# Modulation chunks of the Hyena stage: the contraction over four 32-column groups of TensorE, summed by a selection matmul

## The chip, the cores and the metric

One core of one Trainium2 chip. The metric is the device time of one execution in microseconds; a lower number is better. Three runs of the kernel before are given, and one more execution was recorded by the hardware profiler.

## What is computed

One layer of a hybrid diffusion trunk over 1,024 latent and 128 context tokens of width 1,024. The part that matters here is the modulation, a linear map of two conditioning vectors (latent and context) to six rows of width 1,024 each:

```python
def adaln(cond, w_mod, b_mod):
    return jnp.split(jax.nn.silu(cond) @ w_mod + b_mod, 6, axis=-1)
...
proj = h @ p['w_in'][l]     # its last 3 x 512 columns feed the Hyena mixer
uc = up[:, :-2] * short_w[0] + up[:, 1:-1] * short_w[1] + up[:, 2:] * short_w[2] + short_b
```

`silu(cond) @ w_mod` is a product of a 2 x 1024 matrix with a 1024 x 6144 one. All data are float32.

## The kernel before, in words

The program of each engine is written out by hand and ordered by semaphores. SP's queue issues nearly all loads; waits on it hold back what is behind them.

`w_mod` is taken in 24 chunks of 256 columns (`CHUNK`, `MOD_CHUNKS`). The first eight (`COND_CHUNKS`) are done at the start. The other 16, chunks 8 to 23, are done in the second stage, which also projects the 12 Hyena features of 128 channels (`FEATS`) from six chunks of `w_in` of 256 columns. After each pair of features a group of modulation chunks follows: `MODS_AFTER = (3, 3, 3, 3, 2, 2)`.

Every chunk of either matrix is 1 MB and goes through a ring of two places, `wring` (line 222): the place of a chunk comes free when the product two chunks before it is done. `HY_AT` and `MOD_AT` (lines 380, 381) number the ring's chunks in order: one of `w_in`, then the group's chunks of `w_mod`, then the next of `w_in`. In a group of three, here called m0, m1 and m2, SP (lines 457 to 471) loads m0 during the features; m1 once the second feature's product is there, since it takes the `w_in` chunk's place; m2 after m0's product; the next `w_in` chunk after m1's product; the next group's m0 after m2's product. In a group of two the next `w_in` chunk is loaded after m0's product.

On TensorE (lines 1049 to 1067) a feature is 24 calls of `mm` (8 steps of contraction by 512, 512 and 128 tokens). Then the feature before it is transposed to tokens (`to_tokens`), and after an odd feature follow the products of the group. `modulation` (line 934) multiplies eight 128-row slices of `w_mod` by the two-column `cond_silu` into two rows of a PSUM bank (`mod_bank`, line 368), accumulating over the slices. A float32 call appears in the trace as two weight loads and two matmuls, so a chunk is 16 matmuls and a feature is 48.

ScalarE copies the two rows to one of two places of `mod_ring` (`copy_mod`, line 656). Before it takes a place again it waits until the store of the chunk two before it has landed (`mod_stored`, line 659). GpSimd (lines 569 to 581) loads the piece of the bias, adds it, for chunks 16 to 19 adds 1.0 as well (line 579), and issues the store of the row to DRAM. The next feature, which is the first to write banks 0 to 2 again, waits on TensorE for `mod_copied` of the whole group, so for the copy of its last chunk (line 1055). VectorE convolves each feature over the tokens (lines 1532 to 1538), normalises and rotates one tile of queries and keys, and after the last feature goes on to the Fourier transforms of the Hyena mixer.

Of the kernel before, what the change touches and what calls it, by code (L numbers as in the profile page):

```python
# [19 lines left out]
ALU = mybir.AluOpType  # L20
ACT = mybir.ActivationFunctionType
AX = mybir.AxisListType
# [6 lines left out]
KT = D // P  # L29
# [10 lines left out]
CHUNK = 256  # L40
MOD_CHUNKS = 6 * D // CHUNK
COND_CHUNKS = 2 * D // CHUNK
# [4 lines left out]
MODS_AFTER = (3, 3, 3, 3, 2, 2)  # L47
# [100 lines left out]
def build(nc, I, O):  # L148
    ctx = ExitStack()
    with ctx:  # L150
        SB_COLS = 53000
        PS = ctx.enter_context(nc.psum_tensor("PS", [P, 8 * 512], F32))

        def bank(b, width=512, rows=P, at=0):
            return PS[0:rows, 512 * b + at:512 * b + at + width]
# [11 lines left out]
        def sem(name):  # L167
            if name not in sems:
                sems[name] = ctx.enter_context(nc.semaphore(name))
            return sems[name]  # L170


        keep = Columns(nc, 0, 4096)
        tables = keep.take(4 * P + 32)
        ident, ones, upper, row128 = (tables[:, P * i:P * (i + 1)] for i in range(4))
# [10 lines left out]
        cond_silu = keep.take(16, "p (k c) -> p k c", c=2)  # L186
# [3 lines left out]
        hid_cols = keep.take(P)  # L190
        w1_sb = keep.take(HID)
        col_v = keep.take(8)
        col_q = keep.take(8)
        col_t = keep.take(8)
        col_r = keep.take(16, "p (o i) -> p o i", o=2)
# [28 lines left out]
        w3 = low.take(4 * HW)  # L224
# [13 lines left out]
        U = [top.take(NTILE * HW, "p (t n) -> p t n", t=NTILE) for _ in range(3)]  # L238
        TAIL0 = top.at
        uc = top.take(2 * T, "p (r t) -> p r t", r=2)  # L240
        rope = Columns(nc, 50560, SB_COLS)
        rot = rope.take(NLAT * 2 * HD, "p (t s d) -> p t s d", t=NLAT, s=2)
        qk_work = rope.take(640)
        swap = rope.take(640)
# [122 lines left out]

        def mod_bank(c):

            return bank(6 + c % 2, CHUNK, rows=2) if c < COND_CHUNKS else bank(MOD_PLACE[c], CHUNK, rows=2)  # L370

        def mat(cls, kind):

# [7 lines left out]
        MOD_AT = [*range(COND_CHUNKS), *(HY_AT[c] + 1 + i for c in range(HY_CHUNKS) for i in range(MODS_AFTER[c]))]  # L381

        MOD_PLACE = {COND_CHUNKS + sum(MODS_AFTER[:c]) + i: i for c in range(HY_CHUNKS) for i in range(MODS_AFTER[c])}

        def ring(at):
            return wring[:, at % 2, :, :]

        def ring_count(at):
            return 16 * (at // 2 + 1)
# [8 lines left out]
        def _(sp):  # L398
# [51 lines left out]
            def mods_before(c):  # L450
                return COND_CHUNKS + sum(MODS_AFTER[:c])
# [5 lines left out]
            for c in range(HY_CHUNKS):  # L457
                for i in range(MODS_AFTER[c]):
                    m = mods_before(c) + i
                    if i >= 2:  # L460
                        sp.wait_ge(sem("mod_product"), m - 1)
                    elif i == 1:
                        sp.wait_ge(sem("feature_product"), 2 * (c + 1))
                    elif c:
                        sp.wait_ge(sem("mod_product"), m)
                    else:
                        sp.wait_ge(sem("qkv_product"), QKV_CHUNKS * NTILE)
                    load_w_mod(m)
                if c + 1 < HY_CHUNKS:
                    sp.wait_ge(sem("mod_product"), mods_before(c + 1) - 1)  # L470
                    load_w_in(QKV_CHUNKS + c + 1, HY_AT[c + 1])

            for r in range(3):
# [173 lines left out]
        def _(act):  # L647
# [8 lines left out]
            def copy_mod(c):  # L656
                act.wait_ge(sem("mod_product"), c + 1)
                if c >= COND_CHUNKS + 2:
                    act.wait_ge(sem(f"mod_stored{c % 2}"), 16 * ((c - COND_CHUNKS) // 2))
                elif c >= 2:  # L660
                    act.wait_ge(sem(f"cond_stored{c % 2}"), 16 * (c // 2))
                act.copy(mod_ring[0:2, c % 2, :], mod_bank(c)).then_inc(sem("mod_copied"), 1)  # L662
                if c < COND_CHUNKS:
                    act.wait_ge(sem("mod_copied"), c + 1)
                    act.dma_start(mod_d[:, CHUNK * c:CHUNK * (c + 1)], mod_ring[0:2, c % 2, :]).then_inc(
                        sem(f"cond_stored{c % 2}"), 16)

            def hidden(layer):
                act.wait_ge(sem("arg_ready"), layer + 1)
                dst = h1T if layer == 0 else h2T[0:HID, :]  # L670
                act.activation(dst, arg, ACT.Sin).then_inc(sem("sine_ready"), 1)
# [68 lines left out]
            for p in range(PASSES):  # L740
                m = 7 * p
# [23 lines left out]
                        copy_spectrum(p, SPEC_MID + i // 2)  # L765

            def copy_mods(c):
                for i in range(MODS_AFTER[c]):
                    copy_mod(COND_CHUNKS + sum(MODS_AFTER[:c]) + i)

            def square_qk(t):

# [143 lines left out]
        def _(pe):  # L916
# [17 lines left out]
            def modulation(c):  # L934
                at = MOD_AT[c]
                pe.wait_ge(sem(f"w_loaded{at % 2}"), ring_count(at))
                if c >= 2:
                    pe.wait_ge(sem("mod_copied"), c - 1)
                for k in range(KT):
                    last = mm(mod_bank(c), cond_silu[:, k, :], ring(at)[:, k, :], k == 0, k == KT - 1)  # L940
                last.then_inc(sem("mod_product"), 1)

            def taps(p, i):
                n, (j, d), (o, half) = N_ITEMS * p + i, divmod(i, 2), divmod(p, 2)
                if n >= 2:
                    pe.wait_ge(sem("taps_ready"), n - 1)
                mm(taps_bank(n), h2T[:, P * j:P * (j + 1)], w3_taps(o, half, d)).then_inc(sem("taps_product"), 1)
# [63 lines left out]
            for p in range(PASSES):  # L1011
                m = 7 * p
# [22 lines left out]

            pe.wait_ge(sem("spectrum_copied"), PASSES * N_SPEC)
            pe.wait_ge(sem("qkv_copied"), QKV_CHUNKS * NTILE)

            def to_tokens(f):
                pe.wait_ge(sem("conv_ready"), f + 1)  # L1040
# [8 lines left out]
            for f in range(FEATS):  # L1049
                at = HY_AT[f // 2]  # L1050
                b = 3 * (f % 2)
                pe.wait_ge(sem(f"w_loaded{at % 2}"), ring_count(at))
                if f >= 2:
                    pe.wait_ge(sem("conv_ready"), f - 1)
                    pe.wait_ge(sem("mod_copied"), COND_CHUNKS + sum(MODS_AFTER[:f // 2]))
                for part, (t0, t1) in enumerate(((0, 512), (512, 1024), (1024, T))):
                    for k in range(KT):
                        last = mm(bank(b + part, t1 - t0), ring(at)[:, k, P * (f % 2):P * (f % 2 + 1)], xT[:, k, t0:t1],
                                  k == 0, k == KT - 1)
                last.then_inc(sem("feature_product"), 1)  # L1060
                if f:
                    to_tokens(f - 1)
                if f % 2 == 1:
                    pe.wait_ge(sem("conv_ready"), f)
                    first = COND_CHUNKS + sum(MODS_AFTER[:f // 2])
                    for c in range(first, first + MODS_AFTER[f // 2]):
                        modulation(c)
            to_tokens(FEATS - 1)
            pe.wait_ge(sem("mod_copied"), MOD_CHUNKS)
            pe.wait_ge(sem("mats_loaded"), 32)  # L1070
# [52 lines left out]
            for s in range(10):  # L1123
# [8 lines left out]
                for a in range(4):  # L1132
                    last = turn(bank(b + 2, P, at=P * a),
                                k_split[:, s % 2, a // 2, a % 2, :, :].rearrange("p c d -> p (c d)").bitcast(F32))
# [103 lines left out]
            for i in range(2 * NTILE):  # L1238
                last = mm(bank(4, MAX_BLOCKS), r_hot[:, i, :], r_tok[:, i, :], i == 0, i == 2 * NTILE - 1)
# [5 lines left out]
            with pe.Fori(0, pairs) as i:  # L1245
                for u in range(2):
# [4 lines left out]
                    for k in range(KT):  # L1251
                        last = turn(bank(2 * u + k // 4, P, at=P * (k % 4)), xg[:, u, k:D:KT])
                    last.then_inc(sem("x_transposed"), 1)
                for u in range(2):
                    pe.wait_ge(sem("xT_ready"), 2 * i + u + 1)
                    pe.wait_ge(sem(f"we_loaded{u}"), 32 * i + 32)
                    for g in range(2):
                        for s in range(2):
                            for k in range(KT):
                                last = mm(bank(4 + u, P, at=256 * g + P * s), w_gu[:, u, g, k, s:FF:2], xgT[:, u, k, :],  # L1260
                                          k == 0, k == KT - 1)
                    last.then_inc(sem("gate_up_product"), 1)
                for u in range(2):
                    pe.wait_ge(sem(f"wd_loaded{u}"), 16 * i + 16)
                    pe.wait_ge(sem("hidden_ready"), 2 * i + u + 1)
                    for c in range(2):
                        for s in range(2):
                            last = mm(bank((6, 2)[u] + c), hT[:, u, s, :], w_dn[:, u, s, 512 * c:512 * (c + 1)], s == 0, s == 1)
# [3 lines left out]
        def _(dve):  # L1272
            steps = [0]

            def own(ins):

                steps[0] += 1
                ins.then_inc(sem("dve_step"), 1)
                dve.wait_ge(sem("dve_step"), steps[0])
# [3 lines left out]
            def give(ins, name):  # L1283

                counts[name] = counts.get(name, 0) + 1
                ins.then_inc(sem(name), 1)
                dve.wait_ge(sem(name), counts[name])
# [199 lines left out]
                transform_taps(p)  # L1487


            for lc in range(2):  # L1490
                own(dve.tensor_copy(tap_s[:, 0:4, lc, 0:3], taps[:, 0:4, :]))
                own(dve.tensor_copy(tap_s[:, 0:4, lc, 3], tap_bias[:, 0:4]))
                for o in range(2):
                    f = slice(4 * o + 4, 4 * o + 8)
                    r = col_r[:, o, 4 * lc:4 * lc + 4]
                    own(tt(tap_s[:, f, lc, 0:3], taps[:, f, :], r.unsqueeze(2).broadcast_to([P, 4, 3]), ALU.mult))
                    own(tt(tap_s[:, f, lc, 3], tap_bias[:, f], r, ALU.mult))
# [68 lines left out]
            for s in range(10):  # L1566
# [3 lines left out]
                r = s % 2  # L1570
# [200 lines left out]
            for t in range(NTILE):  # L1771
                a, at = acc[:, t % YN, :], 16 * (t % YN)
# [59 lines left out]
```

## Time and profile before

| | us |
|---|---|
| three runs | 2078.23, 2080.09, 2081.88 (median 2080.09) |
| the profiled execution, its own time | 2078.15 |
| span of that execution in the profile | 2076.3 |
| TensorE matmuls busy in the span | 1581.8 (76%) |
| VectorE busy | 1041.8 (50%) |
| ScalarE busy | 399.2 (19%) |
| GpSimd busy | 281.4 (14%) |
| second stage, first feature to last transposition | about 354 to 634 |

The page counts matmuls as PE and weight loads as PEld. PEclk is the clock that TensorE was granted, as a share of 2.4 GHz: 1.00 is that level, 0.50 is 1.2 GHz. In the chain of waits a DMA counts from its issue to its landing. Times of positions are microseconds from the span's start. A time given for a group of modulation chunks below counts from the issue of m1's load, which is when the second feature's product is done.

### The profile page before, as it was taken

Reading aid. Unit: us, or ns where it says so; the run is one execution under the profiler, and the core shown is the slowest. Engines: PE = TensorE matmul, PEld = TensorE weight load, DVE = VectorE, ACT = ScalarE, POOL = GpSimd, SP = SyncE. Lnnn points to the kernel's source line nnn. Section 1 sums busy time; section 2 is a strip of 40 time slices with the busy share of each in tenths; the row PEclk is TensorE's granted clock in tenths of the full one; section 3 lists DMA queues with packets and bytes.
Section 4 is the critical chain, followed back from the end, with each engine's and each line's share of the span. In section 5 each row is a group of like instructions: output and inputs, shape, how many; then the busy total and the mean of one; then the engine's idle time right before and its main releaser. Section 6 shows DMA issues by size and latency. Waiting matters only on the chain.

```text
span 2076.3 us, 21496 instructions
## 1 busy us (share of the span) xinstructions
PE 1581.8 (76%) x7898; PEld 1121.6 (54%) x7898; DVE 1041.8 (50%) x1823; ACT 399.2 (19%) x774; POOL 281.4 (14%) x263
## 2 busy tenths in 40 slices
PE   4798787999993904818988997999539999999800
PEld 1376575444441401317888886455338888788700
DVE  2457655455527598685665666443341111112187
ACT  1542331010000100104333333011001111111021
POOL 0220220111100000000000000245300000001076
PEclk8798898999996956959998997999659999999955
DMA  7311112222222201129300001111148898888542
GB/s 242 128 56 66 46 52 86 82 82 82 81 73 81 78 20 31 61 81 407 139 1 1 1 1 34 68 61 41 51 181 325 338 348 327 346 344 342 219 176 94
DMA packets 98624, 273.79 MB, mean 132 GB/s; under 512 B 9415, under 2 KB 55063, under 8 KB 85048
## 3 DMA queue, kind: packets, MB, share of 16 engines
q1 hardware_dynamic: 72152, 215.07, 28.4%
q10 hardware_dynamic: 17888, 30.43, 3.9%
q0 software_dynamic: 8512, 27.34, 3.5%
q8 instruction: 43, 0.70, 0.1%
q14 instruction: 29, 0.24, 0.0%
HBM read 207.62 MB, written 65.19 MB: 131 GB/s over the span
## 4 chain that ended last, share of the span: by engine, by line
PE 60%; DVE 23%; DMA 6%; POOL 5%; issue 3%; ACT 2%; SPq 0%; ACTq 0%; POOLq 0%; DVEq 0%
PE PS L918 55%; DVE buffer L1290 11%; PE PS L921 5%; DVE buffer L1303 3%; DMA buffer<-in_w_mod 3%; POOL buffer L566 1%; DMA buffer<-in_x_tok 1%; DVE buffer L1636 1%; DVE buffer L1758 1%; POOL buffer L599 1%; POOL buffer L601 1%; POOL buffer L593 1%; POOL buffer L591 1%; DMA buffer<-in_w_in 1%; DVE buffer L1315 1%
## 5 line engine op out<-in xcount | busy, mean ns | idle before, releaser
L918 PE MATMUL PS<-buffer 128*128 128x128 f32 (+6 forms) x6678 | 1435.4, 375 | 295.0 <-DVE buffer L1290 167.3
L918 PEld LDWEIGHTS PS<-buffer 128*128 128x128 f32 (+2 forms) x6678 | 973.3, 194 | 729.4 <-issue 358.3
L1290 DVE TENSOR_TENSOR buffer<-buffer 128x512 f32<-128x512 f32 (+15 forms) x534 | 323.7, 606 | 36.6 <-ACT buffer L787 9.7
L921 PE MATMUL PS<-buffer 128*128 128x128 f32 x1220 | 180.0, 296 | 88.8 <-DVE buffer L1290 67.1
L921 PEld LDWEIGHTS PS<-buffer 128*128 128x128 f32 x1220 | 153.6, 163 | 113.9 <-issue 92.3
L1290 DVE TENSOR_TENSOR buffer<-PS,buffer 128x256 f32<-128x256 f32 (+2 forms) x135 | 97.7, 724 | 139.6 <-PE PS L918 97.3
L1290 DVE TENSOR_TENSOR buffer<-buffer,PS 128x256 f32<-128x256 f32 (+2 forms) x44 | 19.0, 431 | 260.1 <-ACT buffer L885 244.0
L820 ACT ACTIVATE buffer<-PS,buffer 128x1152 f32<-128x1152 f32 (+1 forms) x72 | 81.1, 1127 | 215.9 <-DVE buffer L1584 215.9
L1584 DVE TENSOR_REDUCE buffer<-PS 128x1 f32<-128x1152 f32 (+1 forms) x72 | 89.2, 1240 | 65.0 <-PE PS L918 64.6
L1303 DVE SCALAR_TENSOR_TENSOR buffer<-buffer 128x512 f32<-128x512 f32 (+5 forms) x119 | 111.6, 938 | 4.1
L591 POOL TENSOR_TENSOR buffer<-buffer 128x1024 f32<-128x1024 f32 x9 | 21.1, 2344 | 483.5 <-DVE buffer L1650 483.5
L566 POOL TENSOR_TENSOR buffer<-buffer 128x256 f32<-128x256 f32 x64 | 46.4, 726 | 245.3 <-ACT buffer L697 240.9
L1534 DVE TENSOR_SCALAR buffer<-PS,buffer 128x1024 f32<-128x1024 f32 (+1 forms) x24 | 21.0, 877 | 99.6 <-PE PS L918 99.2
L1767 DVE COPY buffer<-PS 128x512 f32<-128x512 f32 x34 | 23.5, 692 | 90.8 <-PE PS L918 90.8
L885 ACT ACTIVATE buffer<-PS 128x256 f32<-128x256 f32 x34 | 13.1, 384 | 253.2 <-PE PS L918 253.2
L1614 DVE COPY buffer<-PS 128x640 f32<-128x640 f32 x64 | 52.8, 825 | 7.6 <-PE PS L921 5.7
L611 POOL COPY buffer<-buffer 128x1 int32 x34 | 6.3, 186 | 363.0 <-PE PS L921 314.3
L575 POOL TENSOR_TENSOR buffer<-buffer 2x256 f32<-2x256 f32 x16 | 11.4, 714 | 302.3 <-ACT buffer L662 278.8
L787 ACT COPY buffer<-PS 128x512 f32<-128x512 f32 (+1 forms) x36 | 15.2, 481 | 186.8 <-PE PS L921 186.8
L1758 DVE COPY buffer<-PS 128x1024 f32<-128x1024 f32 x34 | 40.1, 1220 | 14.0 <-PE PS L921 14.0
L1630 DVE TENSOR_SCALAR buffer<-PS,buffer 128x128 f32<-128x128 f32 x36 | 12.6, 351 | 65.7 <-PE PS L921 64.7
L705 ACT COPY buffer<-PS 128x256 f32<-128x256 f32 x88 | 32.2, 366 | 65.2 <-PE PS L918 53.1
(104 smaller groups left out, 735.0 us busy)
## 6 DMA issues: line engine op xcount, KB each, us to landing
buffer<-in_exp_w_gate SPq DMA_DIRECT2D x34, 1024.0 KB, 4.8
buffer<-in_exp_w_up SPq DMA_DIRECT2D x34, 1024.0 KB, 6.9
buffer<-in_exp_w_down SPq DMA_DIRECT2D x34, 1024.0 KB, 8.5
slot_outputs<-buffer SPq DMA_DIRECT2D x5, 5120.0 KB, 39.1
buffer<-in_w_mod SPq DMA_DIRECT2D x24, 1024.0 KB, 5.4
slot_outputs<-buffer ACTq DMA_DIRECT2D x34, 512.0 KB, 8.7
filter_spectra<-buffer ACTq DMA_DIRECT2D x88, 128.0 KB, 1.7
buffer<-filter_spectra SPq DMA_DIRECT2D x22, 512.0 KB, 3.6
```

The source lines that it names most:

```text
L566: pool.tensor_tensor(total, total, sq[:, added % 2, :], ALU.add).then_inc(sem("sq_added"), 1)
L591: pool.tensor_tensor(x1[:, t, :], xnorm, ln1_g, ALU.mult).then_inc(sem("pool_step"), 1)
L705: act.copy(spec_out[:, m % 3, :], spec_bank(m)).then_inc(sem("spectrum_copied"), 1)
L820: act.activation(probs[:, i % 2, 0:n], PS[:, 0:n], ACT.Exp, bias=nmax[:, i:i + 1], scale=1.0, accum_out=psums[:, i:i + 1]).then_inc(sem("e ...
L918: return nc.tensor.matmul(out, lhsT, rhs, start=start, stop=stop)
L921: return nc.tensor.transpose(out, in_, ident)
L1290: return dve.tensor_tensor(out, a, b, op)
L1303: own(dve.scalar_tensor_tensor(out, a, s, b, ALU.mult, op))
L1584: give(dve.tensor_reduce(nmax[:, i:i + 1], PS[:, 0:n], AX.X, ALU.max, negate=True), "max_ready")
L1614: give(dve.tensor_copy(probsT[:, i % 2, 4:9, :], PS[:, 2048:2688].rearrange("p (t n) -> p t n", t=5)), "probsT_d")
L1758: dve.tensor_copy(xgT[:, u, :, :], PS[:, 1024 * u:1024 * (u + 1)].rearrange("p (k n) -> p k n", k=KT)).then_inc(sem("xT_ready"), 1)
L1767: dve.tensor_copy(ybuf[:, u, 512:1024], bank((7, 3)[u])).then_inc(sem("y_d"), 1)
```

## The change

Three things are made once on VectorE, ahead of the short-tap scales: `cond_wide`, the conditioning vectors in 8 slices of 32 columns, of which two hold data and 30 are zero; the zeroing itself; and `part_sum`, a 128 x 2 selection matrix that has a one where a partition is 0 or 1 modulo 32. In `modulation_parts` the eight slices of a chunk go to four column groups of the array, two slices to each, so that four partial sums land on partitions 0, 32, 64 and 96 of a bank. ScalarE copies the whole 128 x 256 of partial sums to SBUF (`copy_parts`, into `w3`, which is no longer needed and has room for four chunks in use), and `sum_parts` multiplies them by `part_sum`, which gives the two rows in the second half of the same bank. All partial products of a group come first on TensorE, then all sums; on ScalarE all copies of parts, then all copies of rows. The waits of SP's loads go by the partial products. GpSimd's program stays as it is. `SB_COLS` grows by 200 columns.

```diff
+        part_sum = keep.take(2)
...
-        rope = Columns(nc, 50560, SB_COLS)
+        cond_wide = Columns(nc, 52928, SB_COLS).take(KT * 32, "p (k m) -> p k m", k=KT)
+        rope = Columns(nc, 50560, 52928)
...
-            return bank(6 + c % 2, CHUNK, rows=2) if c < COND_CHUNKS else bank(MOD_PLACE[c], CHUNK, rows=2)
+            return bank(6 + c % 2, CHUNK, rows=2) if c < COND_CHUNKS else bank(MOD_PLACE[c], CHUNK, rows=2, at=CHUNK)
+
+        mod_parts = w3.rearrange("p (r c) -> p r c", r=8)
...
                     if i >= 2:
-                        sp.wait_ge(sem("mod_product"), m - 1)
+                        sp.wait_ge(sem("parts_product"), m - 1 - COND_CHUNKS)
                     elif i == 1:
                         sp.wait_ge(sem("feature_product"), 2 * (c + 1))
                     elif c:
-                        sp.wait_ge(sem("mod_product"), m)
+                        sp.wait_ge(sem("parts_product"), m - COND_CHUNKS)
...
-                    sp.wait_ge(sem("mod_product"), mods_before(c + 1) - 1)
+                    sp.wait_ge(sem("parts_product"), mods_before(c + 1) - 1 - COND_CHUNKS)
...
+            def copy_parts(c):
+                act.wait_ge(sem("parts_product"), c - COND_CHUNKS + 1)
+                if c >= COND_CHUNKS + 4:
+                    act.wait_ge(sem("mod_product"), c - 3)
+                act.copy(mod_parts[:, c % 4, :], bank(MOD_PLACE[c], CHUNK)).then_inc(sem("parts_copied"), 1)
...
             def copy_mods(c):
-                for i in range(MODS_AFTER[c]):
-                    copy_mod(COND_CHUNKS + sum(MODS_AFTER[:c]) + i)
+                first = COND_CHUNKS + sum(MODS_AFTER[:c])
+                for m in range(first, first + MODS_AFTER[c]):
+                    copy_parts(m)
+                for m in range(first, first + MODS_AFTER[c]):
+                    copy_mod(m)
...
+            def modulation_parts(c):
+                at = MOD_AT[c]
+                pe.wait_ge(sem(f"w_loaded{at % 2}"), ring_count(at))
+                for half in range(2):
+                    for j in range(4):
+                        k = 2 * j + half
+                        last = nc.tensor.matmul(PS[32 * j:32 * j + 32, 512 * MOD_PLACE[c]:512 * MOD_PLACE[c] + CHUNK],
+                                                cond_wide[:, k, :], ring(at)[:, k, :], start=half == 0, stop=half == 1,
+                                                tile_position=(0, 32 * j))
+                last.then_inc(sem("parts_product"), 1)
+
+            def sum_parts(c):
+                pe.wait_ge(sem("parts_copied"), c - COND_CHUNKS + 1)
+                mm(mod_bank(c), part_sum, mod_parts[:, c % 4, :]).then_inc(sem("mod_product"), 1)
...
+            pe.wait_ge(sem("cond_wide_ready"), 1)
...
                     for c in range(first, first + MODS_AFTER[f // 2]):
-                        modulation(c)
+                        modulation_parts(c)
+                    for c in range(first, first + MODS_AFTER[f // 2]):
+                        sum_parts(c)
...
+            own(dve.tensor_reduce(part_sum, ident.rearrange("p (j m) -> p m j", j=4)[:, 0:2, :], AX.X, ALU.add))
+            own(dve.memset(cond_wide, 0.0))
+            give(dve.tensor_copy(cond_wide[:, :, 0:2], cond_silu), "cond_wide_ready")
```

## Rows read from the trace of the kernel before

**Rows 1.** The page: span, engines, and matmul share and clock in 40 slices.
```profile
span 2076.3 us, 21496 instructions
...
PE   4798787999993904818988997999539999999800
...
PEclk8798898999996956959998997999659999999955
```

**Rows 2.** Windows, five groups: length, then busy PE, PEld, DVE, ACT, POOL; PEclk, DMA, GB/s.
```profile
385.94:400.46 14.52, 11.95 (x57) 4.60 (x56) 5.02 (x6) 2.50 (x7) 3.54 (x6) 1.00 0.66 218
433.22:447.92 14.70, 11.95 (x58) 4.60 (x56) 5.02 (x6) 2.50 (x7) 3.53 (x6) 1.00 0.65 215
...
528.05:543.81 15.76, 11.95 (x58) 4.61 (x56) 5.02 (x6) 2.50 (x7) 5.30 (x8) 1.00 0.61 201
576.56:586.83 10.27, 8.34 (x42) 3.30 (x40) 5.02 (x6) 1.99 (x5) 1.76 (x3) 1.00 0.64 205
619.61:632.50 12.89, 9.73 (x42) 3.59 (x40) 5.02 (x6) 1.63 (x4) 1.76 (x3) 0.87 0.66 240
```

**Rows 3.** Chain of waits in the first group: start, duration, what.
```profile
385.94 5.45 DMA buffer<-in_w_mod
...
391.44 3.63 PE PS L918 x16
...
395.09 5.27 DMA buffer<-in_w_in
```

**Rows 4.** Timeline of the first group, and ScalarE's copy of the second group's last chunk.
```profile
387.28 3.62 PE L918 MATMUL PS<-buffer 128*2 128x256 f32 x16
...
390.94 0.36 ACT L662 COPY buffer<-PS 2x256 f32<-2x256 f32 x1 [3.28 <-PE PS L918]
...
392.47 0.56 POOL L581 DMA_DIRECT2D mod_rows<-buffer  x1 [0.30 <-POOL buffer L575]
...
447.41 0.36 ACT L662 COPY buffer<-PS 2x256 f32<-2x256 f32 x1 [4.79 <-PE PS L918]
...
447.92 1.52 PE L918 MATMUL PS<-buffer 128*128 128x512 f32 x3 [0.54 <-ACT buffer L662]
```

**Rows 5.** Timeline and forms: small products, and the copy of a 128 x 256.
```profile
1368.70 1.98 PE L918 MATMUL PS<-buffer 128*128 128x36 f32 x16 [1.10 <-ACT buffer L863]
...
L705 ACT COPY buffer<-PS 128x256 f32<-128x256 f32 x88 | 32.2, 366 | 65.2 <-PE PS L918 53.1 <-DMA filter_spectra<-buffer 12.0
```

**Rows 6.** Stores of modulation rows, issue to landing: all; then those at 449.0 and 397.7.
```profile
DMA to landing us min/median/max: 1.6/3.9/28.8
...
DMA to landing us min/median/max: 4.0/4.0/4.0
...
DMA to landing us min/median/max: 2.9/2.9/2.9
```

**Rows 7.** Windows: two loads in flight.
```profile
621.00:627.00 6.00, 3.57 (x17) 1.23 (x16) 3.70 (x6) 0.69 (x3) 1.60 (x3) 1.00 1.04 355
```

**Rows 8.** Windows, TensorE alone: busy time and granted clock.
```profile
624.60:627.00 2.40, 0.00 (x0) 1.00 0.98 373
627.50:630.40 2.90, 2.90 (x7) 0.50 0.57 240
536.95:539.60 2.65, 0.00 (x0) 1.00 0.69 217
```

**Rows 9.** Timeline and windows of a restart after a long idle stretch.
```profile
317.82 6.79 PE L918 MATMUL PS<-buffer 128*128 128x256 f32 x16 [8.11 <-DVE buffer L1290]
...
323.00:324.00 1.00, 0.91 (x4) 0.48 (x3) 0.97 (x2) 0.37 (x1) 0.00 (x0) 0.86 0.49 169
```

**Rows 10.** Chain of waits, last group.
```profile
619.61 7.83 DMA buffer<-in_w_mod
...
627.48 5.08 PE PS L918 x16
```

**Rows 11.** Timeline: VectorE's first work after its operations ahead of the features.
```profile
354.24 0.43 DVE L1299 TENSOR_SCALAR buffer<-buffer 128x512 f32<-128x512 f32 x1 [12.61 <-PE PS L918]
```

More of the change, by code:

```diff
@@ L150, in build @@
     with ctx:
-        SB_COLS = 53000
+        SB_COLS = 53200
         PS = ctx.enter_context(nc.psum_tensor("PS", [P, 8 * 512], F32))
```

## The prediction

> **What bounds the kernel now.** I read the page first. TensorE's matmuls are busy in nine tenths of most slices between 350 and 620 us, at the full clock [rows 1]. That is the second stage, where the change is. A busy engine doesn't yet say that TensorE sets its length, so the windows came next, one for each group of modulation chunks [rows 2]. A group of three takes 14.52 to 15.76 us from m1's load to the next feature, and TensorE is busy for 11.95 of them. The rest is waiting for data.
>
> The chain of waits says which product counts. In the first group it runs from the end of the features to the landing of m1 (5.45 us), m1's product (3.63), then the next `w_in` chunk (5.27) [rows 3]. So one product in three is on the path. m0's lies under the load of m1, and m2's ends just ahead of the landing of `w_in`. The second group ends otherwise: the last thing before the feature is ScalarE's copy of m2's rows, at 447.41, and the feature starts 0.51 later [rows 4]. Two paths end within half a microsecond of each other, one through SP's loads and one through m2's copy. Whatever shortens one product must be followed down both.
>
> **The price of the partial products.** A chunk's product takes 3.62 us now: 16 matmuls of 256 columns at 0.226 [rows 4]. No row shows column groups. The floor, four groups fully overlapped, is a quarter of that, 0.9. The ceiling is no overlap, 3.62. Between them: each call is two matmuls in a row on the same column group, and I expect these not to overlap each other, only the second of one call with the first of the next. Then 16 matmuls take 9 turns of 0.226, or 2.0 us. The nearest row of small products has the same size: 16 matmuls of 36 columns with 128-column weights take 1.98 [rows 5], which weight loads and issue alone cost there. I take 2.0 and keep 0.9 and 3.62 for the range.
>
> The page "TensorEngine Tiling (Array Packing)" of the Trainium skill (section Tiling Modes) says that a change of tiling mode drains TensorE; no row here shows one. "TensorE: Matmul & The Clock Gate" of the Trainium skill (Part 3) has 2.38 times for three column groups. By that ratio a chunk would take about 1.5 us, an estimate, and the sum below would be some 4 us smaller.
>
> **The loads of a group of three**, in us from m1's load, with 2.0 for a product. m0's parts run from 1.34 to 3.34. m2's load, issued then, lands at 8.8 by the usual 5.4; m1's load at 5.45 plus a megabyte at 355 GB/s (3.0) [rows 7] would allow 8.5. m1's parts run from 5.5 to 7.5. The `w_in` chunk is issued at 7.55 and lands at 12.9, where it now takes 14.4. By this path alone each group would gain 1.6.
>
> **The new wait.** The sums stand behind all the parts. Sum 0 needs only m0, but waits in TensorE's queue for m2's parts, which end at 10.85; a sum is two matmuls, 0.45, so it ends at 11.35. Only then can ScalarE copy m0's rows. From that copy to GpSimd's store is 1.53 now (390.94 to 392.47) [rows 4]. The store takes 1.6 to land at the least, 3.9 in the median, and longer with a load in flight [rows 6]; two stores in this stage took 4.0 and 2.9. The new one, issued at 12.9, comes 2.0 after the load of the next m0; the 4.0 was 1.6 after a load and the 2.9 was 2.6 after one. I take 3.5, so it lands at 16.4.
>
> m2 uses the place of `mod_ring` that m0 had. Its copy waits for that store, and the next feature waits for its copy: 0.55 more [rows 4]. The feature starts at 16.95, where it starts at 14.62 now (the first two groups are 14.52 and 14.70 [rows 2], and the third is like them). Today m0's product ends 4.96 us into the group and m2's at 14.0, so the store has landed long before anyone asks. Behind the waiting copy on ScalarE stand only the square of queries and keys and token copies, and VectorE, busy for 5.0 of such a group's 14.5 us [rows 2], has room.
>
> In the fourth group GpSimd's extra operation is on the path too. Its busy time there is 5.30 for 3.54, with two chunks in the window, so 0.9 for one [rows 2], and about 1.0 with its gap: 18.0 against 15.76. So the order costs 2.3 in each of four groups, **+9.2**.
>
> **The clock.** At 624.57 TensorE falls idle; it is at 1.00 until 627 and at 0.50 when it goes on at 627.48, after 2.9 us, and stays there for 2.9 us more [rows 8]. That product took 5.08 for 3.62 [rows 10]. An idle stretch of 2.65 us in the fourth group left the clock at 1.00 [rows 8]. After a longer pause, the restart at 317.82 ran until about 323.1 at the lower level, 5.3 us [rows 9]. New groups have TensorE idle from the last sum (about 12.3) to 16.95, 4.6 us, behind a stretch in which it works for a third of the time. I expect the feature to start at 1.2 GHz and to stay there for 3.0 to 5.3 us, which costs half of that, 1.5 to 2.7. With some cold parts before it, 2.3 a group: **+9.2**.
>
> **The groups of two.** In the fifth, m0's parts end at 3.34 in place of 4.96 and `w_in` is issued then; it lands by 8.8, but m1's parts, both sums and two copies end at about 9.4, against 10.27 [rows 2]. That is -0.9, and a cold piece gives it back: 0. In the last, TensorE idles 4.5 us for m1, which shares the queue with the inverse matrices (7.83 [rows 10]), and starts cold: 4.0 for the parts, 0.5 for ScalarE's copy, which nothing covers here, and 0.9 for the sum, 5.4 against 5.08, and slower transpositions behind it: **+0.6**.
>
> **What is hidden.** VectorE's three new operations (some 0.7 us) come ahead of an idle stretch of 12.6 us [rows 11]; were that cover gone they would cost their 0.7. The 16 copies of parts, 0.37 each [rows 5], lie under loads, except the last one above and part of the gap before sum 1. SP's queue has the same loads in the same order. The first eight chunks are untouched.
>
> **Sum.** 9.2 + 9.2 + 0 + 0.6 = +19.0 us. The profiled execution's own time is 2078.15 (span 2076.3 and 1.9 around it), which gives 2097.2; it is 1.9 below the median of the three runs. I say **2098**.
>
> **Rivals.** *(a) The groups don't overlap.* Each chunk then takes 3.62, m2's parts end at 14.05, the store lands at 19.6 and the feature starts at 20.15: +5.5 a group, 22 for four, 9 for the clock, 2 in the last two: 2112. For it: float32 calls, and weight loads in between. Against: the four groups are independent. 13 in 100.
>
> *(b) The clock holds.* Waits as forecast, no cold start: +9.2, and in the last two groups -0.9 and (2.0 + 0.5 + 0.45 for 5.08) -2.1, 2084 to 2086. For it, the 2.65 us without a fall. Against it, 2.9 us with one. 12 in 100.
>
> *(c) Faster: the wait for the store is short.* At 0.9 a chunk, m2 lands at 8.45, its parts end at 9.35 and sum 0 at 9.85. With the smallest landing time, 1.6, the feature starts at 9.85 + 1.53 + 1.6 + 0.55 = 13.5, 1.1 sooner than now. Four groups give -4.4 and the last two -2.8: 2073. The point of decision is a landing time of 2.7 at full overlap, and the clock must hold as well. For it, the 1.6 in the row; against, that a load is always in flight. 6 in 100. A balance of such a gain with a little of the clock's loss, within 0.2%, gets 7.
>
> **The numbers.** My forecast, order and clock together with a product between 0.9 and 2.6, has 62 in 100; at 0.9 it gives about 2089. 0.2% of this time, 4.2 us, is about what can be told from no change. Only (c) is faster, so 0.06, 0.07 and 0.87. The range 2084 to 2113 holds (a), (b) and the forecast's own bounds, and leaves out (c) and the balance.
>
> **What would show it.** For the order: L662's third copy in a group waiting for a store, and the feature's wait laid on it, 16 to 17 us into the group. For the clock: 0.5 in the first microseconds of features 2, 4, 6 and 8, and more than 48 matmuls' 15.8 us there. For the overlap: 16 matmuls of 128*32 in about 2 us. The forecast is wrong if the feature is released by `in_w_in` at about 13 us, or if PEclk stays at 1.00 throughout the stage.

## The result: the order made a wait for a store, and the wait cost the clock

The changed kernel takes 2100.05 us in the median of five runs (2094.68 to 2102.73), the kernel before 2078.79. The ratio is 1.0094, with a 95% interval of 1.0076 to 1.0112: slower by some 21 us, where 2098 was forecast. The traces below are of one execution each. Executions of one kernel differ by up to some 10 us here, so a trace can stand some us off its kernel's median; where it matters the text says so. The page of the changed kernel, beside [rows 1]:

```profile
span 2098.2 us, 21582 instructions
## 1 busy us (share of the span) xinstructions
PE 1571.4 (75%) x7930; PEld 1116.0 (53%) x7930; DVE 1044.3 (50%) x1826; ACT 404.9 (19%) x790; POOL 283.7 (14%) x263
...
PEclk8898898889897865958999898899659999999955
```

TensorE is busy for 10 us less than before, and the span is 22 us longer. The six groups, from m1's load to the next work on TensorE, beside [rows 2] (length, then busy PE, PEld, DVE, ACT and POOL, granted clock, DMA share, GB/s; the fifth window begins 0.96 early, the load was issued at 597.36):

```profile
387.36:404.89 17.53, 7.81 (x63) 2.99 (x62) 5.02 (x6) 3.61 (x10) 2.11 (x4) 0.78 0.73 240
440.51:457.40 16.89, 7.78 (x63) 3.06 (x62) 5.02 (x6) 3.62 (x10) 2.10 (x4) 0.73 0.77 249
492.37:509.43 17.06, 7.72 (x64) 2.98 (x62) 5.02 (x6) 3.62 (x10) 2.11 (x4) 0.80 0.76 246
543.88:561.60 17.72, 7.55 (x63) 2.97 (x62) 5.02 (x6) 3.61 (x10) 2.98 (x5) 0.79 0.72 238
596.40:607.09 10.69, 6.77 (x55) 3.23 (x53) 5.02 (x6) 2.74 (x7) 0.71 (x1) 0.75 0.67 217
642.30:653.37 11.07, 5.57 (x46) 2.28 (x45) 5.02 (x6) 2.38 (x6) 0.08 (x1) 0.69 0.73 277
```

TensorE works for 7.7 of 17.3 us in a group of three, where it worked for 11.95 of 14.5 to 15.8, and the clock is no longer 1.00. The chain of waits through the first group (start, duration, what) stands against [rows 3]:

```profile
388.76 1.05 PE PS L962 x16
...
389.83 6.85 DMA buffer<-in_w_mod
...
396.72 1.93 PE PS L962 x16
398.66 0.85 PE PS L931 x2
399.53 0.37 ACT buffer L666
...
400.04 0.72 POOL buffer L579
400.77 0.29 issue
401.06 3.25 DMA mod_rows<-buffer
404.35 0.04 issue
404.39 0.37 ACT buffer L666
404.76 0.14 issue
404.89 18.62 PE PS L931 x48
```

Here everything is to be seen. m0's parts take 1.05 us. The 1.93 us of m2's parts isn't the 2.0 that I forecast come true: it is the same product at half the clock. The load that follows m0's parts is m2's, its parts (L962) and sum 0 (L931) come next, and then the round trip of m0's row: copied by ScalarE (L666), added to by GpSimd (L579), stored, landed, and only now is m2's row copied. The feature starts 0.50 after that copy does. And the 48 matmuls of that feature take 18.62 us where they took 15.76. The timeline of the same stretch names the wait and shows that the next `w_in` chunk, issued at 394.61, isn't what TensorE waits for:

```profile
393.08 1.49 PE L962 MATMUL PS<-buffer 128*32 128x256 f32 x16 [3.31 <-DMA buffer<-in_w_mod]
394.61 0.54 SPq L404 DMA_DIRECT2D buffer<-in_w_in  x1
...
404.39 0.36 ACT L666 COPY buffer<-PS 2x256 f32<-2x256 f32 x1 [3.65 <-DMA mod_rows<-buffer]
...
404.89 1.19 PE L931 MATMUL PS<-buffer 128*128 128x512 f32 x1 [4.02 <-ACT buffer L666]
```

The clock as the sums begin and just ahead of the feature (busy PE, PEld, DVE, ACT, POOL, clock, DMA share, GB/s), and then in windows of TensorE alone: in the pause, at the start of the feature and later in it (busy time, clock, DMA share, GB/s):

```profile
398.70:399.50 0.80, 0.80 (x3) 0.26 (x2) 0.00 (x0) 0.37 (x1) 0.00 (x0) 0.50 0.89 298
...
403.70:404.85 1.15, 0.00 (x0) 0.00 (x0) 0.00 (x0) 0.46 (x2) 0.30 (x1) 0.56 0.00 1
...
401.00:404.00 3.00, 0.00 (x0) 0.97 0.79 268
405.00:410.00 5.00, 5.00 (x6) 0.50 0.02 3
411.00:420.00 9.00, 9.00 (x22) 1.00 0.00 0
```

So the clock was low when the sums began (0.50), was up again in the pause (0.97), and fell a second time at the pause's end (0.56), before the feature began. The feature's slow start is that second fall. Below, a feature is called cold when it begins at half the clock and takes 17.2 us or more, and warm when it takes 15.76 to 15.79.

**The account.** By the two profiles the last transpositions start 20.9 us later (653.37 for 632.50). The four groups of three are longer by 3.01, 2.19, 2.43 and 1.96, together 9.6. The features behind them take 18.62, 17.97, 17.45 and 18.77 for 15.76, together 9.8 more. The fifth group is 0.5 shorter, and the feature behind it 2.4 longer. The last group is 1.8 shorter. The stage began 1.4 later; the other kernels below begin it between 384.1 and 388.3, so I take that for scatter and not for an effect of the change. The sum is 20.9. The spans differ by 21.9; the last 1.0 lies behind this stage.

Not every cold feature has a store's wait ahead of it. In the fifth group, which has only two chunks and no wait for a store, the feature starts 0.55 after the last sum and still takes 18.22:

```profile
604.86 1.70 PE PS L931 x4
...
607.09 18.22 PE PS L931 x48
```

### The profile page after: what moved, and what is told of

Its sections match the earlier page's. It is cut to its first block, busy times and chain, and to the rows that moved or that the text cites. A ratio compares the mean times of both kernels' runs of the same rounds, so it can differ in the third digit from the quotient of the medians.

```text
span 2098.2 us, 21582 instructions
## 1 busy us (share of the span) xinstructions
PE 1571.4 (75%) x7930; PEld 1116.0 (53%) x7930; DVE 1044.3 (50%) x1826; ACT 404.9 (19%) x790; POOL 283.7 (14%) x263
## 4 chain that ended last, share of the span: by engine, by line
PE 59%; DVE 22%; DMA 7%; POOL 5%; issue 3%; ACT 2%; ACTq 0%; SPq 0%; POOLq 0%; DVEq 0%
PE PS L931 53%; DVE buffer L1321 10%; PE PS L934 5%; DVE buffer L1334 3%; DMA buffer<-in_w_mod 3%; DMA buffer<-in_x_tok 1%; POOL buffer L570 1%; DVE buffer L1670 1%; DVE buffer L1792 1%; POOL buffer L603 1%; POOL buffer L605 1%; POOL buffer L595 1%; POOL buffer L597 1%; PE PS L962 1%; DMA mod_rows<-buffer 1%
## 5 line engine op out<-in xcount | busy, mean ns | idle before, releaser
L931 PE MATMUL PS<-buffer 128*128 128x128 f32 (+5 forms) x6454 | 1403.4, 378 | 296.3 <-DVE buffer L1321 167.3
L931 PEld LDWEIGHTS PS<-buffer 128*128 128x128 f32 (+2 forms) x6454 | 960.0, 198 | 713.9 <-issue 392.3
L579 POOL TENSOR_TENSOR buffer<-buffer 2x256 f32<-2x256 f32 x16 | 12.5, 782 | 323.6 <-ACT buffer L666 305.3
L1792 DVE COPY buffer<-PS 128x1024 f32<-128x1024 f32 x34 | 40.1, 1220 | 14.1 <-PE PS L934 14.1
L962 PE MATMUL PS<-buffer 128*32 128x256 f32 x256 | 23.6, 501 | 29.3 <-DMA buffer<-in_w_mod 29.3
```

The lines of the kernel that those rows point to most:

```text
L931: return nc.tensor.matmul(out, lhsT, rhs, start=start, stop=stop)
L962: last = nc.tensor.matmul(PS[32 * j:32 * j + 32, 512 * MOD_PLACE[c]:512 * MOD_PLACE[c] + CHUNK], cond_wide[:, k, :], ring(at)[:, k, :], st ...
L1792: dve.tensor_copy(xgT[:, u, :, :], PS[:, 1024 * u:1024 * (u + 1)].rearrange("p (k n) -> p k n", k=KT)).then_inc(sem("xT_ready"), 1)
```

## The experiments

Theory 1 is that of the prediction: the wait for the store and the clock. Its rivals: the clock alone; the wait alone; column groups that are slow in themselves. Each kernel was run beside the kernel before, whose median in the three series was 2079.45, 2080.79 and 2079.61. The changed kernel itself was measured only in the series of the result, beside a 2078.79; differences from its 2100.05 compare two series and can be 1 to 2 us off.

**Four places for the rows.** The second stage's rows go to the unused half of the array of partial sums, and four semaphores count their stores:

```diff
-                if c >= COND_CHUNKS + 2:
-                    act.wait_ge(sem(f"mod_stored{c % 2}"), 16 * ((c - COND_CHUNKS) // 2))
+                if c >= COND_CHUNKS + 4:
+                    act.wait_ge(sem(f"mod_stored{c % 4}"), 16 * ((c - COND_CHUNKS) // 4))
...
-                act.copy(mod_ring[0:2, c % 2, :], mod_bank(c)).then_inc(sem("mod_copied"), 1)
+                act.copy(mod_row(c), mod_bank(c)).then_inc(sem("mod_copied"), 1)
```

> The changed kernel, with four places in place of two for the modulation rows of the second stage (in the unused half of the array of partial sums), so that no copy waits for a store. Theory 1 (wait for the store and clock, about half of the loss each): a group of three starts its next feature 13.5 to 14 us after m1's load in place of 16.9 to 17.7, the next features still run 17.5 to 18.8 us for 15.76, the time is 2086 (2083 to 2090). Theory 2 (the clock alone costs, the wait for the store only lies over a load that is as late): 2098 to 2101.

Measured: 2072.9 us (2069.45 to 2078.2), ratio to the kernel before 0.9975 [0.9963, 0.9987]. That is 27 us below the changed kernel, twice what was expected (2086). The features start as forecast, 13.8 us into the first group, but they are not cold. The chain in the first group:

```profile
394.80 1.94 PE PS L965 x16
396.73 1.91 PE PS L934 x6
...
398.66 0.37 ACT buffer L669
...
399.17 3.24 PE PS L934 x7
```

and two windows, one before and one across the feature's start (busy PE, PEld, DVE, ACT, POOL, clock, DMA share, GB/s):

```profile
393.00:398.00 5.00, 3.20 (x20) 1.22 (x21) 0.00 (x0) 1.08 (x3) 0.00 (x0) 0.52 0.71 221
398.00:404.80 6.80, 6.26 (x16) 2.66 (x15) 4.56 (x15) 1.36 (x3) 3.58 (x6) 1.00 0.48 155
```

m2's parts still run at 1.2 GHz (1.94 us), but the sums now follow the parts at once, the feature starts 0.5 to 1.0 us after the sums, and the clock is back at 1.00 when the feature begins. All five features behind a group take 15.76 to 15.79 us. So my two terms were not two: the wait makes the pause in front of the feature, and the pause makes the cold start. Theory 1 as I had put it, each with half of the loss, falls; the wait is the cause of nearly all of it. Two things qualify this. The fifth feature is warm here too, which gives back 2.4 us that no wait for a store had cost. And since this kernel holds everything of the change but the two places, its 2072.9 shows that the column groups, the copies of parts and the sums cost nothing on balance.

**Useless matmuls in the pauses**, the wait kept:

```diff
+                    fill = (6, 4, 8) if f < 8 else (6, 0) if f < 10 else (10, 0)
...
                         modulation_parts(c)
+                        if c + 1 < first + MODS_AFTER[f // 2]:
+                            for _ in range(fill[c - first]):
+                                mm(bank(2, CHUNK, at=CHUNK), ident, xT[:, 0, 0:CHUNK])
...
                         sum_parts(c)
+                    for _ in range(fill[-1]):
+                        mm(bank(7, CHUNK), ident, xT[:, 0, 0:CHUNK])
```

> The changed kernel with matmuls of no use in TensorE's idle stretches (256 columns each, 6 after m0's parts, 4 after m1's, 8 after the sums; 10 after m0's parts in the last group). The wait for the store stays. Theory 1: granted clock 1.00 through the groups, features at 15.8 us, starts at 16 to 16.5 us into a group, time 2084 (2081 to 2088). If the useless matmuls only push the real ones back and the clock costs nothing: 2100 or more.

Measured: 2082.5 us (2078.13 to 2084.97), ratio 1.0020 [1.0011, 1.0030], so 17.5 below the changed kernel. The chain shows the store still there ahead of the features, and the clock back in all of them but one:

```profile
400.75 3.65 DMA mod_rows<-buffer
...
404.99 15.76 PE PS L931 x48
...
449.19 5.00 DMA mod_rows<-buffer
...
454.77 17.45 PE PS L931 x48
```

The one cold feature, at 454.77, stands behind the longest landing, 5.0 us, which the matmuls did not fill: TensorE is idle for 2.6 us before it, and for 1.1 to 1.6 before the four warm ones.

**Both edits.**

> Both edits: four places for the rows, and useless matmuls after m0's (6; last group 10) and m1's parts (4), none after the sums. Theory 1: both losses are gone and the gain of the shorter product is left, 2 us a group: 2070 (2066 to 2075), faster than the kernel before at 2079. If the two losses were one and the same time counted twice: 2080 to 2086.

Measured: 2065.6 us (2064.42 to 2066.75), ratio 0.9944 [0.9927, 0.996]: below both kernels, and 34.5 below the changed one, where the two edits alone gave 27.1 and 17.5. That is 0.4 under the expected range. The losses overlap, as the first run says. What bounds a group is now the path through SP's loads that the prediction had followed first, m1's load, its parts, and `w_in`:

```profile
384.90 5.52 DMA buffer<-in_w_mod
...
390.47 1.11 PE PS L965 x16
...
391.60 5.54 DMA buffer<-in_w_in
...
397.18 4.99 PE PS L934 x11
```

The four features behind groups of three take 15.79. The fifth takes 17.48, though useless matmuls stand ahead of it too; its pause is 2.0 us, a wait for `w_in`.

**Each sum one chunk after its parts**, two places as before:

```diff
                         modulation_parts(c)
+                        if c > first:
+                            sum_parts(c - 1)
-                    for c in range(first, first + MODS_AFTER[f // 2]):
-                        sum_parts(c)
+                    sum_parts(c)
```

> The changed kernel with each sum and each copy of rows one chunk after its parts and no longer behind all parts of the group: m0's sum follows m1's parts. Two places for the rows as before. Theory 1: m0's store is issued at about 9.5 us and lands at 13, under m2's load and parts, so the time comes near that of four places: 2087 (2083 to 2091). If the store's landing isn't what the feature waited for: 2098 to 2101.

Measured: 2078.6 us (2072.92 to 2082.32), ratio 0.9999 [0.9986, 1.0011]. The loss is gone, with the same work in another order. It came 8 us under what I expected. The trace, of an execution of 2074.6, shows that the groups of three take 13.0 to 14.0 us up to the feature, where the kernel before takes 14.5 to 15.8, and that two of the five features are warm. In the first group the copy of m2's row no longer waits for a store, and its feature takes 15.76. In the next three the store is still on the chain, though sooner in the group, and the features are cold (17.45, 17.45 and 17.89). The second group:

```profile
440.45 3.69 DMA mod_rows<-buffer
...
444.73 17.45 PE PS L932 x48
```

**The order alone, on the kernel before.** No column groups, no sums; the rows of a group are copied once all its products are done. TensorE's own wait for copies, which would now never end, is dropped in this stage:

```diff
+                act.wait_ge(sem("mod_product"), first + MODS_AFTER[c])
                 for i in range(MODS_AFTER[c]):
-                    copy_mod(COND_CHUNKS + sum(MODS_AFTER[:c]) + i)
+                    copy_mod(first + i)
...
-                if c >= 2:
+                if 2 <= c < COND_CHUNKS:
                     pe.wait_ge(sem("mod_copied"), c - 1)
```

> The kernel before with one change of order alone: ScalarE copies a group's rows only when all products of the group are done. The products stay undivided (3.62 us), no sums, no copies of parts, two places for the rows. Theory 1 (the order with two places makes the wait, whatever the product): m2's copy waits for m0's store, the feature starts 19 to 20 us into a group of three for 14.6, and after the idle stretch it runs 17.5 to 18.8 us for 15.76: 2107 (2102 to 2112). If the column groups themselves cost the time: 2079 to 2081.

Measured: 2112.3 us (2108.92 to 2114.4), ratio 1.0158 [1.0141, 1.0175], 5 more than expected and 0.3 outside the range. The first feature starts 20.2 us into its group, where 19 to 20 was expected. The chain has the same pair of rows:

```profile
400.62 3.97 DMA mod_rows<-buffer
...
405.18 18.80 PE PS L920 x48
```

The next three features take 18.12, 17.82 and 18.80.

So the order and the two places make the loss, whichever way the product is done. With the quick product it is smaller: the products of the first group end 11.3 us into it, and here 14.1.

**The same with useless matmuls**, nine calls behind the last product of each group of three:

```diff
+                    if f < 8:
+                        pe.wait_ge(sem("mod_copied"), first + 1)
+                        for _ in range(9):
+                            mm(bank(7, CHUNK), ident, xT[:, 0, 0:CHUNK])
```

> The kernel before with the late copies of rows (the order alone, 2112.3 us) and nine useless matmuls of 256 columns (4.1 us) in each of the four idle stretches ahead of a feature. It prices the clock without any column group. Theory: the waits stay, the four features run 15.8 us for 17.8 to 18.8, so 10.5 us less, 2102 (2098 to 2105). If the lower clock of those features has another cause than the idle stretch: 2110 to 2114.

Measured: 2101.4 us (2098.98 to 2103.92), ratio 1.0104 [1.0087, 1.0122]. All four features are at 15.76. This prices the cold starts with no column group in the kernel: 10.9 us for four by the medians, 10.5 by the four features of the two traces. The windows of TensorE (busy time, granted clock, DMA share, GB/s), first without and then with these matmuls:

```profile
399.20:405.10 5.90, 0.00 (x0) 0.66 0.54 179
405.20:411.50 6.30, 6.30 (x8) 0.52 0.01 1
```

```profile
399.20:405.10 5.90, 5.31 (x24) 1.00 0.73 243
405.20:411.50 6.30, 5.06 (x12) 1.00 0.01 1
```

**Four places in the kernel before**, a control of that edit.

> The kernel before with four places for the rows in place of two and nothing else: a control of that edit. In the kernel before no copy waits for a store, so both theories say no difference, 2078 to 2080; a gain here would mean that the gain of four places in the changed kernel isn't all the wait's.

Measured: 2080.7 us (2077.49 to 2083.05), ratio 1.0002 [0.9991, 1.0013]. No difference. The edit gains only where a copy waits.

**All slices on one column group.**

```diff
-                        last = nc.tensor.matmul(PS[32 * j:32 * j + 32, ...
-                                                cond_wide[:, k, :], ring(at)[:, k, :], start=half == 0, stop=half == 1,
-                                                tile_position=(0, 32 * j))
+                        last = nc.tensor.matmul(PS[0:32, ...
+                                                cond_wide[:, k, :], ring(at)[:, k, :], start=k == 0, stop=k == 7,
+                                                tile_position=(0, 0))
...
-            own(dve.tensor_reduce(part_sum, ident.rearrange("p (j m) -> p m j", j=4)[:, 0:2, :], AX.X, ALU.add))
+            own(dve.tensor_copy(part_sum, ident[:, 0:2]))
```

> The changed kernel with all eight slices of a chunk on one column group (columns 0 to 31, accumulated over eight), the copy of 128 x 256 and the sum as before, the sum taking partitions 0 and 1 alone. It shows what the overlap of groups is worth. Expected: a chunk's product 3.6 us in place of 1.07, m2's parts end 2.5 to 5 us later, the feature starts at 20 to 21 us, 2112 (2106 to 2118). If it is a matter of issue and not of groups, the product stays near 1.07 to 2.0 and the time at 2100.

Measured: 2112.7 us (2106.56 to 2112.91), ratio 1.0157 [1.014, 1.0174]. It is my rival (a), which I had put at 2112: the first feature starts 20.3 us into its group, where (a) said 20.15. The trace is of an execution of 2106.56, 6 below the median, and its features are less cold than (a) assumed. The timeline of the first group:

```profile
394.55 3.64 PE L962 MATMUL PS<-buffer 128*32 128x256 f32 x16 [1.38 <-DMA buffer<-in_w_mod]
...
404.35 17.30 PE L931 MATMUL PS<-buffer 128*128 128x512 f32 x48 [4.87 <-ACT buffer L666]
```

A product of 32 columns on one group takes 3.64 us, the undivided one with two columns 3.62. So 32 weight columns in place of two cost 0.02 us, and the overlap of the four groups is worth 3.64 to 1.07.

**The two slices of a group one behind the other.**

```diff
-                for half in range(2):
-                    for j in range(4):
+                for j in range(4):
+                    for half in range(2):
```

> The changed kernel with the two slices of a column group issued one right behind the other (four matmuls in a row on one group) in place of one slice to each group in turn. If a matmul that must wait for its own group holds up those behind it, 16 matmuls take 13 turns of 0.226, 2.9 us, and the time is 2104 to 2108. If each group takes its matmuls on its own, the product stays at 1.07 us and the time at 2100.

Measured: 2100.5 us in two runs (2097.62 and 2103.41), ratio 1.0098 [1.0076, 1.0121], the time of the changed kernel. m0's parts on the timeline:

```profile
388.11 1.09 PE L962 MATMUL PS<-buffer 128*32 128x256 f32 x16
```

So four matmuls in a row on one group don't hold up those of the next group.

**Both cures of the wait.**

> The changed kernel with both cures of the wait: four places for the rows, and each sum and copy one chunk after its parts. With four places no copy waits for a store, so the order of the sums is worth only the sum or two that no longer stand behind m2's parts, under 1 us in a group of three: 2070 (2067 to 2073) where four places alone gave 2072.9.

Measured: 2073.1 us (2071.35 to 2077.45), ratio 0.9976 [0.9962, 0.999], no different from four places alone (2072.9). The feature behind the fifth group is cold in its trace, 18.33 us, where it was warm with four places alone. That may take back what the earlier sums give; no run separates the two.

**m0 undivided, m1 and m2 on column groups, four places.** `modulation(first)` in place of `modulation_parts(first)`, its row copied directly, and the waits of SP's loads by its own product.

> Four places for the rows, and in each group m0's product undivided as in the kernel before (3.62 us, it lies under m1's load and keeps TensorE at work), m1 and m2 on four column groups. m2's load then goes out at 5.0 us in place of 2.4 and lands at 10.5; m2's row is copied at about 13.4, which sets the feature: 1.2 us sooner than in the kernel before, and features at 15.8. Expected 2074 (2070 to 2078), so slower than with useless matmuls and divided m0 (2065.6).

Measured: 2080.1 us (2077.93 to 2085.07), ratio 1.0001 [0.999, 1.0012], 6 more than expected. The idea, to let a slow product keep the clock up, did not work out. The trace is of an execution of 2084.66, 4.6 above the median, so it shows more of the loss than the median has. The timeline of the first group:

```profile
393.24 1.07 PE L974 MATMUL PS<-buffer 128*32 128x256 f32 x16 [0.46 <-DMA buffer<-in_w_mod]
398.47 1.93 PE L974 MATMUL PS<-buffer 128*32 128x256 f32 x16 [4.16 <-DMA buffer<-in_w_mod]
```

m2's load goes out only behind m0's slow product, so the pause moves to between m1's and m2's parts, 4.16 us, and three of five features are cold (18.29, 17.61 and 18.78 us). The first feature came 14.8 us into its group, not 13.4. The second group has the same order and nearly the same pauses (4.34 in place of 4.16, then 0.55 before the feature in both), and its feature takes 15.76 where the first takes 18.29.

## Why the prediction was right, and where it wasn't

The time was right, 2098 for 2100.05, and so were the mechanism and its place. That it came within 2 us is in part luck: terms of the sum were off in both directions. Point by point:

- **The new wait**: right. Forecast at 2.3 a group of three and 9.2 in all, measured 9.6 (3.01, 2.19, 2.43 and 1.96). That it hangs on the order of sums and copies with two places is shown from three sides: four places (-27.1), earlier sums (-21.5), and the late copies in the kernel before (+31.5).
- **The clock**: right in size for the four features, 9.2 forecast (with some cold parts), 9.8 measured. Each feature loses 1.7 to 3.0, two of them more than the 2.7 that I had as the most. (The restart in [rows 9] was at half clock until about 323.3 by its 0.86, so for 5.5 us and not 5.3.) The prediction drew this term from the pause that the wait makes. In my expectation of the run with four places I forgot this and left the features cold without the wait, and there it failed: with four places the pause before the feature is gone and the feature is warm, though TensorE has the same work in the rest of the group.
- **The price of the parts**: the step of the prediction that failed. I let each call's two matmuls hold up the next group's, and took 2.0 us; it is 1.07 at 2.4 GHz (the first group's m0, in a window with the clock at 1.00). In the sum this hardly showed, because two other terms went the other way. m2's parts run at the lower clock and take 1.93 or 1.94, and m1's take 1.49 and 1.93 in the first two groups. And m2's load, issued 2.5 us after m1's, landed 6.85 after its issue, where I had taken 5.4. So m2's parts end 11.3 us into the first group by the trace, with 10.85 forecast. That is nearly the right number out of wrong terms.
- **The store's landing**: 3.5 assumed, 3.25, 3.61, 3.32 and 2.34 on the chain.
- **What no term had**: the stage that began 1.4 us later, and 1.0 behind it.
- **The groups of two**: forecast 0 and +0.6; measured +1.9 and -1.8. In the fifth I had seen only "a cold piece", and its feature takes 18.22 us. In the last, m1's parts take 1.93 and the sums with their gap 1.46, 3.4 in all, where I had 5.4. Beside the forecast the one is 1.9 over and the other 2.4 under, so these two mistakes cancelled.
- **Rivals**: (a) is what one column group gives, 2112.7, and it isn't what the hardware does here. (b) falls with the 0.50 in the features. (c) needed a landing under 2.7 in every group and a warm clock; only one group had such a landing, 2.34, with GpSimd's extra operation before it.
- **The ratio for three column groups**, by which a chunk would take about 1.5 us, an estimate ("TensorE: Matmul & The Clock Gate" of the Trainium skill, Part 3), was nearer than my 2.0: four groups are 3.4 times one here, 3.64 to 1.07. The drain on a change of tiling mode, which "TensorEngine Tiling (Array Packing)" of the Trainium skill states (section Tiling Modes), costs nothing that the trace shows: m0's parts start 0.26 us after the last transposition starts (388.44 to 388.70), and the undivided product did the same (the transposition at 387.02, the product at 387.28, [rows 4]).

Still open: why a feature is cold behind a short pause. In the thirteen traces the 17 features behind the longest pauses, 3.3 to 6.2 us, are all cold. Behind shorter ones the outcome is mixed: 2.6 us before a cold feature with the useless matmuls, 2.8 before a warm one with both cures of the wait, and only 0.55 before the cold fifth feature of the changed kernel. The two alike groups of the last run, one cold and one warm, say that the pause and the work before the feature don't settle it by themselves. Open too is how the groups might be kept warm without useless work.

## What to carry to other kernels

When a product is cut short, follow both what it released and what it kept busy. Here the 3.6 us product lay under a load and cost little, and the new order put a store's whole round trip, 5 us from the sum's end to the landing, between two stages, only because a ring had two places. Before moving several producers ahead of their consumers, count the places of every ring behind them.

A pause of several us in front of a long run of matmuls is paid twice: once as the pause and again as a start at half the clock, 1.5 to 3.0 us each behind the pauses of 3.7 to 6.2 us here. Removing the wait removed both, and useless matmuls only the second.

## What the runs showed of the hardware

- Four column groups overlap nearly fully for float32 calls, in either order of issue: 1.07 and 1.09 us for 16 matmuls of 256 columns at the full clock, where a quarter of the 3.64 on one group is 0.91. I had expected the order of issue to bind.
- Matmuls of no use held the clock: 5.31 us busy of 5.90 at 1.00, where the idle stretch had 0.66 in the mean and the next 6.3 us 0.52.
- The granted clock came back and was lost again within one group: 0.50 as the sums began, 0.97 from 401 to 404 with TensorE idle, 0.56 from 403.70 to 404.85.
- TensorE busy for 3.20 of 5 us at half clock was followed by a warm feature in the first group with four places, 0.54 us after the sums. It is no rule: the fifth feature of the changed kernel was cold with 0.55 us there.
